# x laid out channel-major by the launch, and low weights on VectorE in the second memory's pass of a two-block kernel

## The reference, cut to what matters

```python
def rms_norm(x, g):
    x32 = x.astype(jnp.float32)
    y = x32 * lax.rsqrt(jnp.mean(x32 * x32, axis=-1, keepdims=True) + RMS_EPS)
    return (y * g.astype(jnp.float32)).astype(x.dtype)

def memory_cross_attention(h, mem_n, wq, wkv, wo):
    ...
    k, v = jnp.split(mem_n @ wkv, 2, axis=-1)
    ...
```

## Time and profile before

| | us |
|---|---|
| median of 3 runs | 3284.67 (3283.84 to 3285.05) |
| the profiled execution | 3283.11 |
| its span in the profile | 3281.3 |

### The profile page before, as it was taken

The page is one execution under the profiler, slowest core; times in us unless marked ns, Lnnn a source line. Parts: engine busy times, 40 slices in busy tenths (PEclk is TensorE's granted clock), DMA queues, the critical chain, the costliest instruction groups (busy, mean ns, idle before and its releaser), DMA issues.

```text
span 3281.3 us, 39121 instructions
## 1 busy us (share of the span) xinstructions
PE 3261.5 (99%) x14911; PEld 2691.1 (82%) x14911; DVE 783.6 (24%) x1251; ACT 1085.1 (33%) x1668; POOL 1381.2 (42%) x593
## 2 busy tenths in 40 slices
PE   9999999999999999999999999999999999999999
PEld 8877788887888878888888888888888888888887
DVE  3574321013124444300111101111111134300201
ACT  6542323233246444322223323333222222222332
POOL 7643333433443433444443343334444444444443
PEclk9999999999999999999999999999999999999999
DMA  8522323333433422333333333233333333333342
GB/s 284 174 77 71 84 65 88 87 82 106 116 121 91 129 72 78 84 102 97 89 97 83 90 89 89 78 90 96 97 96 96 96 97 92 101 97 97 103 159 97
DMA packets 536619, 331.02 MB, mean 101 GB/s; under 512 B 17196, under 2 KB 511412, under 8 KB 535220
## 3 DMA queue, kind: packets, MB, share of 16 engines
q1 hardware_dynamic: 522228, 304.82, 32.9%
q10 hardware_dynamic: 14272, 24.52, 2.2%
HBM read 316.71 MB, written 12.58 MB: 100 GB/s over the span
## 4 chain that ended last, share of the span: by engine, by line
PE 66%; issue 23%; POOL 10%; DVE 0%; ACT 0%; POOLq 0%; ACTq 0%; DVEq 0%
PE proj L700 55%; POOL w_lo L679 10%; PE s L1487 3%; PE proj L1487 1%; PE t L1487 1%; PE s L1185 1%; PE t L725 1%; PE t L1185 1%; PE proj L1185 0%; PE s L1382 0%; PE s L1470 0%; PE t L700 0%; PE t L846 0%; PE s L1346 0%; PE s L991 0%
## 5 line engine op out<-in xcount | busy, mean ns | idle before, releaser
L679 POOL TENSOR_TENSOR w_lo<-raw,w_hi 128x1024 fp32r<-128x1024 f32 x564 | 1379.1, 2456 | 1874.2 <-ACT w_hi L1526 1848.0
L700 PE MATMUL proj<-ht_hi,w_hi 128*128 128x512 f32 x3424 | 1356.7, 396 | 5.8 <-DVEq L3073 3.4
L700 PE MATMUL proj<-ht_hi,w_lo 128*128 128x512 f32 x3424 | 1334.4, 390 | 0.0
L700 PE MATMUL proj<-ht_lo,w_hi 128*128 128x512 f32 x3424 | 1333.4, 389 | 0.0
L1526 ACT ACTIVATE w_hi<-raw 128x1024 fp32r<-128x1024 f32 x528 | 543.8, 1054 | 867.2 <-PE proj L700 703.1
L700 PEld LDWEIGHTS proj<-ht_hi,w_hi 128*128 128x128 f32 x3424 | 643.4, 188 | 144.7 <-issue 7.9
L700 PEld LDWEIGHTS proj<-ht_hi,w_lo 128*128 128x128 f32 x3424 | 642.9, 188 | 135.7
L700 PEld LDWEIGHTS proj<-ht_lo,w_hi 128*128 128x128 f32 x3424 | 643.6, 188 | 134.5 <-issue 4.8
L700 PE MATMUL proj<-yh,w_hi 128*128 128x512 f32 x368 | 143.2, 389 | 0.0
L700 PE MATMUL proj<-yl,w_hi 128*128 128x512 f32 x368 | 143.2, 389 | 0.0
L700 PE MATMUL proj<-yh,w_lo 128*128 128x512 f32 x368 | 143.2, 389 | 0.0
(11 more groups left out here) (580 smaller groups left out, 2931.3 us busy)
## 6 DMA issues: line engine op xcount, KB each, us to landing
raw<-in_w_in_dram SPq DMA_DIRECT2D x404, 512.0 KB, 3.8
raw<-in_w_out_dram SPq DMA_DIRECT2D x64, 512.0 KB, 3.9
raw<-in_xa_wkv_dram SPq DMA_DIRECT2D x16, 512.0 KB, 7.0
raw<-in_w_mem_kv_dram SPq DMA_DIRECT2D x16, 512.0 KB, 3.5
raw<-in_w_br_gla_dram SPq DMA_DIRECT2D x16, 512.0 KB, 3.9
raw<-in_w_br_pool_dram SPq DMA_DIRECT2D x16, 512.0 KB, 3.9
mem_tok<-in_mem_dram SPq DMA_DIRECT2D x8, 512.0 KB, 7.4
x_tok<-in_x_dram ACTq DMA_DIRECT2D x4, 1024.0 KB, 7.3
```

Of the source, the lines that this page charges most:

```text
L679: pool.tensor_tensor(w_lo[:, slot, :], raw[:, slot, :], w_hi[:, slot, :].bitcast(F32), ALU.subtract).then_inc(lo_done, 1)
L700: ins = pe.matmul(dst, w, x[:, kt, c0:c1], start=first and n == 0 and m == 0, stop=last and n == len(kts) - 1 and m == 2)
```

## The change

The launch hands over a second copy of x, transposed to channels x tokens (`x_ch`, 16 x 128 x 512). The kernel's use of it, and what moves with it:

- **SP** loads it in four pieces of 1 MB into `x_t`, between the loads of the second pass's halves: piece 0 ahead of half 16, piece 1 behind half 18, piece 2 behind half 21, piece 3 behind half 24. Ahead of piece 0 it waits for `mem_ready[0]` and `in_ss`, ahead of piece 1 for `mem_ready[1]`.
- **TensorE** no longer transposes x. The token-major load and its sums of squares stay.
- **VectorE** makes the low parts of the halves 16 to 31. It scales x out of `x_t`. The keys of the first memory move behind the pass; the values go to ScalarE.
- **GpSimd** makes the low parts of the halves 0 to 15, then waits for 32 to be done, and goes on with 32.
- **ScalarE** loses the copies to `x_t` and the writes to `x_spill`, which is gone; the later residual is read from `x_ch`.

```diff
+            def x_tiles(c):
+                sp.dma_start(x_t[:, 4 * c:4 * c + 4, :], a["x_ch"][4 * c:4 * c + 4].rearrange("k p t -> p k t")
+                             ).then_inc(xt_in[c], 16)
+
             for j in range(KT, 2 * KT):
+                if j == KT:
+                    sp.wait_ge(mem_ready[0], KT)
+                    sp.wait_ge(in_ss, 8)
+                    x_tiles(0)
                 kv_rows(j)
+                if j == KT + 2:
+                    sp.wait_ge(mem_ready[1], KT)
+                    x_tiles(1)
+                elif j in (KT + 5, KT + 8):
+                    x_tiles((j - KT + 1) // 3)
...
-            with pool.Fori(0, NH // RING) as i:
+            def low_rows(i):
                 for slot in range(RING):
                     pool.wait_ge(hi_done, i * RING + slot + 1)
                     pool.tensor_tensor(w_lo[:, slot, :], raw[:, slot, :], w_hi[:, slot, :].bitcast(F32),
                                        ALU.subtract).then_inc(lo_done, 1)
+
+            with pool.Fori(0, KT // RING) as i:
+                low_rows(i)
+            pool.wait_ge(lo_done, 2 * KT)
+            with pool.Fori(2 * KT // RING, NH // RING) as i:
+                low_rows(i)
...
                 kv_rows(1, kt)
-                if kt:
-                    x_cols(kt - 1)
-            x_cols(KT - 1)
...
-            pe.wait_ge(xt_x, KT - 2)
             unit(H4["lru"], 0, Q2["lru"], 0, fresh=HT_X)
...
+            pe.wait_ge(k1_kept, 4)
             pe.wait_ge(mlg_ready, 1)
...
-            act.activation(v1[:, :, 0, :], proj[0][:].rearrange("p (h n) -> p h n", n=P), ACT.Copy, scale=r_in[:, 0:1]
-                           ).then_inc(bank_free[0], 1)
+            for blk in range(2):
+                act.activation(v1[:, :, blk, :], proj[blk][:].rearrange("p (h n) -> p h n", n=P), ACT.Copy,
+                               scale=r_in[:, blk:blk + 1]).then_inc(bank_free[blk], 1)
...
                 act.wait_ge(norm_t, k + 1)
+                act.wait_ge(half_done, KT + k + 1)
                 act.activation(ht_hi[:, k, :], x_n[k % 2][:], ACT.Copy).then_inc(norm_hi, 1)
-                act.activation(x_t[:, k, :], X_BANK[k % 4][:], ACT.Copy).then_inc(xt_x, 1)
-                if k % 4 == 3:
-                    act.wait_ge(xt_x, k + 1)
-                    act.dma_start(x_spill[k - 3:k + 1].rearrange("k p t -> p k t"), x_t[:, k - 3:k + 1, :]).then_inc(spilled, 16)
...
-                act.dma_start(n_x[u][:], x_spill[u]).then_inc(tile_in[u], 16)
+                act.dma_start(n_x[u][:], a["x_ch"][u]).then_inc(tile_in[u], 16)
...
-            dve.wait_ge(half_done, KT)
-            dve.wait_ge(in_rec, 1)
-            mem_values(0).then_inc(bank_free[1], 1)
-            dve.wait_ge(r_mem_kept, 1)
-            mem_keys(0)
+            def w_low(j):
+
+                dve.wait_ge(hi_done, j + 1)
+                dve.tensor_tensor(w_lo[:, j % RING, :], raw[:, j % RING, :], w_hi[:, j % RING, :].bitcast(F32), SUB
+                                  ).then_inc(lo_done, 1)
+
             scaled_params()
+            dve.wait_ge(lo_done, KT)
+            for j in range(KT, KT + 3):
+                w_low(j)
             dve.wait_ge(r_x_kept, 1)
...
             for k in range(KT):
-                dve.wait_ge(xt_pe, k + 1)
+                if k + 3 < KT:
+                    w_low(KT + k + 3)
+                dve.wait_ge(xt_in[k // 4], 16)
                 if k >= 2:
                     dve.wait_ge(ht_ready, HT_X + k - 1)
-                dve.scalar_tensor_tensor(x_n[k % 2][:], X_BANK[k % 4][:], col("mix_norm_g", k), r_x[:], MUL, MUL
+                dve.scalar_tensor_tensor(x_n[k % 2][:], x_t[:, k, :], col("mix_norm_g", k), r_x[:], MUL, MUL
                                          ).then_inc(norm_t, 1)
...
             dve.wait_ge(half_done, 2 * KT)
-            mem_values(1)
+            mem_keys(0)
             mem_keys(1)
-            dve.wait_ge(spilled, 64)
```

More of the change, by code:

```diff
@@ L214, in build @@
         x_in, weights_in = [sem(f"x_in{t}") for t in range(NT)], sem("weights_in")
-        spilled, out_done = sem("spilled"), sem("out_done")
+        xt_in = [sem(f"xt_in{c}") for c in range(4)]
+        out_done = sem("out_done")
         tile_in = [sem("tile_in0"), sem("tile_in1")]
@@ L219, in events @@
             return Events(sem(name), names)
-        x_spill = nc.dram_tensor("x_spill", (KT, P, T), F32, kind="Internal").ap()
         x3_spill = nc.dram_tensor("x3_spill", (T, D), F32, kind="Internal").ap()
@@ L750, in mem_cols @@
                            ).then_inc(mem_t[x], 1)
-            def x_cols(k):
-                if k == 0:
-                    for t in range(NT):
-                        pe.wait_ge(x_in[t], 16)
-                if k < 2:
-                    pe.wait_ge(bank_free[k], 1)
-                elif k < 4:
-                    pe.wait_ge(k1_kept, k - 1)
-                else:
-                    pe.wait_ge(xt_x, k - 3)
-                transposes(X_BANK[k % 4], [x_tok[:, t, k * P:(k + 1) * P] for t in range(NT)]).then_inc(xt_pe, 1)
             def kv_rows(x, kt):
@@ L1598, in _ @@
             act.wait_ge(half_done, KT)
-            act.activation(v1[:, :, 0, :], proj[0][:].rearrange("p (h n) -> p h n", n=P), ACT.Copy, scale=r_in[:, 0:1]
-                           ).then_inc(bank_free[0], 1)
+            for blk in range(2):
+                act.activation(v1[:, :, blk, :], proj[blk][:].rearrange("p (h n) -> p h n", n=P), ACT.Copy,
+                               scale=r_in[:, blk:blk + 1]).then_inc(bank_free[blk], 1)
             def x_tile(k):
                 act.wait_ge(norm_t, k + 1)
+                act.wait_ge(half_done, KT + k + 1)
                 act.activation(ht_hi[:, k, :], x_n[k % 2][:], ACT.Copy).then_inc(norm_hi, 1)
-                act.activation(x_t[:, k, :], X_BANK[k % 4][:], ACT.Copy).then_inc(xt_x, 1)
-                if k % 4 == 3:
-                    act.wait_ge(xt_x, k + 1)
-                    act.dma_start(x_spill[k - 3:k + 1].rearrange("k p t -> p k t"), x_t[:, k - 3:k + 1, :]).then_inc(spilled, 16)
             for kt in range(KT):
                 w_high(KT + kt + 4)
-                if kt:
-                    x_tile(kt - 1)
-            x_tile(KT - 1)
+                x_tile(kt)
             act.wait_ge(half_done, 2 * KT)
             act.wait_ge(ht_ready, HT_X + KT)
-            act.activation(v2[:, :, 0, :], S[0][:].rearrange("p (h n) -> p h n", n=P), ACT.Copy, scale=r_in[:, 2:3])
+            for blk in range(2):
+                act.activation(v2[:, :, blk, :], S[blk][:].rearrange("p (h n) -> p h n", n=P), ACT.Copy,
+                               scale=r_in[:, 2 + blk:3 + blk])
             def squares(src, dst, n, gain=1.0, added=None):
@@ L1902, in wout_iter @@
                     if x_back:
-                        act.dma_start(n_x[u][:], x_spill[n + 2]).then_inc(tile_in[u], 16)
+                        act.dma_start(n_x[u][:], a["x_ch"][n + 2]).then_inc(tile_in[u], 16)
                     squares(xy[:, n, :], n_sq[:], n + Z_X1)
@@ L2494, in mem_keys @@
                                             rows, MUL)
[L2495 to L2507 removed]
+                    ins.then_inc(k1_kept, 1)
+            def w_low(j):
+                dve.wait_ge(hi_done, j + 1)
+                dve.tensor_tensor(w_lo[:, j % RING, :], raw[:, j % RING, :], w_hi[:, j % RING, :].bitcast(F32), SUB
+                                  ).then_inc(lo_done, 1)
             scaled_params()
+            dve.wait_ge(lo_done, KT)
+            for j in range(KT, KT + 3):
+                w_low(j)
             dve.wait_ge(r_x_kept, 1)
@@ L3425 @@
         args[name] = nc.dram_tensor(f"in_{name}_dram", x.shape, _mybir.dt.from_np(x.dtype), kind="ExternalInput").ap()
+    arrays["in_x_ch_dram"] = x = _np.ascontiguousarray(inputs["x"][0].T.reshape(KT, P, T))
+    args["x_ch"] = nc.dram_tensor("in_x_ch_dram", x.shape, _mybir.dt.from_np(x.dtype), kind="ExternalInput").ap()
     out = nc.dram_tensor("out_0_dram", (1, T, D), F32, kind="ExternalOutput").ap()
```

9 lines of the change are left out of this document (1 added, 8 removed).

## The result

| | before | changed |
|---|---|---|
| median of 17 runs each | 3283.68 us | 3289.94 us |
| lowest | 3281.39 | 3283.2 |
| the profiled execution | 3283.11 | 3283.2 |

The ratio is 1.0018, with a 95% interval of 1.0012 to 1.0025. The changed kernel is 6.3 us longer: inside the range of 3281.5 to 3291.0, 2.5 us above the forecast of 3287.4, and within 0.2% of before. The forecast stood on a median of 3 runs of before, 3284.67 us; over 17 runs it is 3283.68, 1.0 us lower. So the difference that the change makes was forecast as +2.75 us and measured as +6.3. (Three disturbed runs, one of the changed kernel at 5515 us, one of experiment 5 at 9079 us and one of the kernel before at 5523 us, are left out of ratios and ranges; the medians are over all runs.)

What follows compares the result with a forecast made beforehand. TensorE, busy nearly all the time, was taken as the bound. Its terms, -6.86 + 3.15 + 3.46 + 3.0 = +2.75 us, put on the base median of 3284.67, gave 3287.4 us, range 3281.5 to 3291.0.

Steps and rivals of the forecast that it cites:

- steps of 2.82 us: Second memory's pass on TensorE: each step without transposes takes 2.82 us, against 3.25 us with four.
- transposes gone: TensorE, second step of the pass to first lru unit: all 64 transposes of x leave, gain 6.86 us.
- first wait: TensorE ahead of the norm's rows, held through SP's queue, half 16 and ScalarE's diagonals: cost 3.15 us, 0.1 to 5.25.
- clock behind it: TensorE's granted clock drops to 0.50 after each of the two new waits: 1.5 us each, 3.0 us together.
- second wait: TensorE ahead of the second memory's pass, held by VectorE's order until its first low half is ready: cost 3.46 us.
- half 16 lands at 54.4 + 5.2 + 1.35 = 60.95: SP's queue: last split at 54.4, then 5.2 us for x's megabyte and 1.35 us for half 16.
- Half 19: The tight load inside the pass: split by 79.3, wanted by TensorE at 81.0, so in time by 1.7 us.
- SP's wait bites little: Rival at SP's queue: half 16 lands with x, so that wait and its clock loss vanish; 3282.9 us, chance 0.11.
- The clock stays up: Rival: no clock drop in one or both waits of TensorE; 3284.4 to 3285.9 us, chance 0.30.
- Both hidden: Rival: both TensorE waits are hidden and the full 6.86 us gain arrives; 3277.8 us, chance 0.04.
- become the bound: Rival in the pass: VectorE's longer subtraction makes it set the steps, +1.6 us on the forecast; 3289.0 us, chance 0.03.
- starve the ring: Rival on SP's queue: x's megabytes delay the halves behind them, +11.2 us; 3295.8 us, chance 0.07.

Runs made afterwards that it cites:

- experiment 5: Changed kernel with halves 16 to 18 loaded ahead of SP's wait and x's piece 0, and GpSimd making all low halves, VectorE none; 3282.55 us.
- A: The first profiled execution of the changed kernel, the lowest of its 17 runs; 3283.2 us.
- experiment 1: The changed kernel run again unaltered, for a second profile nearer the median; 3289.88 us, ratio 1.0018 against before.
- B: The profiled execution of experiment 1, the unaltered changed kernel near its median; span 3288.2 us.
- experiment 6: Changed kernel with x's first megabyte moved behind half 18, SP's wait left ahead of half 16; 3283.14 us.
- experiment 7: Changed kernel with 24 unread transposes of a constant on TensorE ahead of the norm's rows and 24 ahead of the second pass; 3286.05 us.
- experiment 8: Experiment 3 with SP's wait on mem_ready[1] moved from ahead of half 19 to behind half 21, and piece 1 behind half 19; 3282.33 us.
- experiment 3: Changed kernel with GpSimd also making the low halves 16 to 19, VectorE the other twelve of the pass; 3288.21 us.
- experiment 2: Changed kernel with only SP's queue reordered: halves 16 to 18 load ahead of its wait and x's piece 0; 3281.96 us.
- experiment 4: Changed kernel with the edits of experiment 2 and experiment 3 together; 3276.9 us, ratio 0.9979 against before.

## Why the prediction was right, and where its sizes were off

**The mechanism held; the sizes did not all.** Two waits came at the two places named, with the releasers named, a clock drop behind each (in A behind the second alone), steps of 2.82 us, no wait inside the pass, and hardly anything different behind the first `lru` unit: +7.17 us there and +6.9 at the end of the span in experiment 1, -0.58 and -0.2 in A.

| term | forecast | execution A | execution B (experiment 1) |
|---|---|---|---|
| transposes gone | -6.86 | -6.95 | -6.95 |
| first wait | +3.15 | +1.16 | +6.19 |
| clock behind it | +1.5 | 0 | +2.65 |
| second wait | +3.46 | +3.76 | +3.76 |
| clock behind it | +1.5 | +1.45 | +1.52 |
| sum | +2.75 | -0.58 | +7.17 |

**The time landed well in part by luck.** The terms sum to +2.75 us where the medians differ by 6.3, short by 3.5; that the time is off by only 2.5 comes from the base, taken 1.0 us too high (3284.67 for 3283.68). In B the first wait is 6.19 us, above the 5.25 that the forecast gave as its upper end, and the clock behind it 2.65 for 1.5. The time stayed under 3291.0 because that bound had room for other costs that did not come, and for the high base; with the base of 3283.68 it would have been 3290.0, and the median is 3289.94.

**Transposes.** Right to 0.1 us. VectorE's subtraction is 1.22 to 1.23 us, as taken.

**First wait: the mis-sized term.** The step "half 16 lands at 54.4 + 5.2 + 1.35 = 60.95" has two parts. The 6.55 us from release to landing measured 6.65 (52.25 to 58.90) in A, but 8.1 to 8.4 in the other four of the table, 1.8 more than forecast in B. The megabyte itself landed 5.4 and 5.5 us behind its issue in the two executions of the changed kernel, for 5.2 taken. What was too small is the 1.35 behind it: I priced half 16 as if it had the queue for itself once x was through. Three halves stand behind x and travel at the same time, 2.6 MB at some 400 GB/s in all, and in experiment 1 half 16 was ready only 63.93 - (55.58 + 5.5) = 2.85 us behind x. This says how half 16 can be late, not why it is late in B and not in A: the same four transfers were in flight in both. The three halves landed 6.2, 8.5 and 9.2 us behind their issues in A and 7.9, 8.6 and 9.4 in B, so the last came nearly alike and half 16's place in the burst differed; why stays open. That the megabyte is what delays it is shown by experiment 6, where half 16 landed 3.8 us behind its issue. The other part is the starting point, 55.58 in B for 54.4, 1.2 us more; 1.2 and 1.8 make the 3.0 by which the wait was missed. The 54.4 was read from one execution of before, where ScalarE's lag happened to be middling (half 10 at 37.73). The lag varies by over 3 us between executions, and a wait that is put on a lagging engine takes it along. The forecast gave such a dependence no term.

**Clock behind the first wait.** 1.5 was taken from a wait of 3.4 us. Behind 6.1 us it cost 2.65 (2.84 by experiment 7). The other two profiles with a long first wait lie between. From the norm's rows to the pass experiment 8 takes 71.96 - 64.29 = 7.67 us behind a wait of 4.45, and experiment 3 takes 73.85 - 65.67 = 8.18 behind 5.87, where before takes 5.94: 1.73 and 2.24 us. The length of the wait does not settle it, though: behind the second wait, 3.97 us in four profiles, the clock cost 1.34 (experiment 2), 1.45 (A), 1.52 (B) and 2.56 us (experiment 6).

**Second wait.** 3.76 for 3.46. VectorE's subtraction ends at 69.40 + 1.22 = 70.62 and TensorE starts at 70.88, 0.26 later where I had put 0.05; the last 0.1 is the end of the memory's splits.

**Half 19.** In time by 80.90 - 78.20 = 2.7 us, forecast 1.7. Experiment 3 showed what the sum didn't say: this margin existed only because the second wait held TensorE back. As soon as that wait was gone, half 19 was 3.2 us late, some 1.1 of it because GpSimd's subtraction takes 2.35 us for VectorE's 1.23.

**The rivals.** "SP's wait bites little" (3282.9) is what happened in A, by another cause than the one given: not because half 16 landed with x, but because SP was released at 52.25, 2.15 us ahead of the 54.4 taken. "The clock stays up" happened at the first wait there. "Both hidden" is experiment 4: 3276.9 us measured for 3277.8 forecast, or -6.7 against before for -6.86. VectorE did not become the bound in A, B or experiment 4, and the four megabytes did not starve the ring there. In experiment 3 the second one, with the wait ahead of it, did hold up half 19.

## What to carry to other kernels

These are lessons from this one kernel, not rules. A wait that is put into a queue costs as much as what stands behind it in that queue is needed: read on to the transfers behind it, and count every one in flight when pricing the landing of the first, not only the one ahead. Put new transfers behind the loads that someone waits for; here that order alone was worth 7.9 us, more than the work that the change saved. And take the starting point of a new wait from several executions: an engine's lag that used to be hidden comes through when another queue is made to wait for it.

## What the runs showed of the hardware that was not expected

- The length of a standstill alone did not decide the clock. It stayed at 1.00 behind 3.18 us without work in experiment 7, where TensorE had transposed for 2.78 us right ahead of them. It fell behind 3.17 us in experiment 3, behind 3.97 us in four profiles, and in experiment 5 behind 1.79 us, where TensorE had worked without a gap since 104.66 (the eleven matmuls from 115.15 to 119.33 took 4.18 us instead of 11 x 0.23 = 2.53). The 1.55 us of idle ahead of 104.66 had cost nothing at the clock. Experiment 3, then experiment 5:

```profile
85.86 0.50 PE L779 MATMUL s<-w_hi,ht_hi 128*128 128x512 f32 x1 [3.17 <-POOL w_lo L692]
88.00:90.00 2.00, 2.00 (x12) 0.50 0.99 340
```

```profile
117.00:119.00 2.00, 2.00 (x6) 0.50 0.74 217
```

- What a drop of the clock cost was not fixed by the wait either: 1.34, 1.45, 1.52 and 2.56 us behind the same 3.97 us in four profiles, 1.73 behind 4.45, 2.24 behind 5.87, and 2.65 to 2.84 behind 6.1. What decides it was not tried.
- VectorE beside GpSimd was slower by up to a factor of 4.3 (0.68 to 2.90 us), on a small operation of 128x64 even more. In experiment 4 it took 2.03 us, ending as GpSimd's subtraction ended (69.04), where the changed kernel's took 0.18:

```profile
67.06 2.03 DVE L2472 TENSOR_SCALAR par<-par 128x64 f32<-128x64 f32 x1
...
66.63 2.41 POOL L694 TENSOR_TENSOR w_lo<-raw,w_hi 128x1024 fp32r<-128x1024 f32 x1 [1.52 <-ACT w_hi L1554]
```

  It cost nothing there, since TensorE no longer waits for VectorE at that place.
